# A third kind of expert pass in a mixture-of-experts kernel: the second block of at most 64 tokens holds its high and low parts side by side

## The reference, cut to what matters

```python
h = xb @ w_up[e] + b_up[e]                    # 1024 -> 2048
g = jnp.minimum(h[:, :D_FF], SWIGLU_LIMIT)
lin = jnp.clip(h[:, D_FF:], -SWIGLU_LIMIT, SWIGLU_LIMIT)
act = g * jax.nn.sigmoid(SWIGLU_ALPHA * g) * (lin + 1.0)
y = act @ w_down[e] + b_down[e]               # 1024 -> 1024
```

```
 76 208 143 145 198  80 185  99  48 294  84 119 154  72 229  41
 55 173  73  66  67 162 287  91  11 192 164  69 174  69 178  90
```

## Time and profile before

| | us |
|---|---|
| median of three runs | 2473.09 |
| profiled execution, its own time | 2474.64 |
| its span, first to last instruction | 2472.9 |
| of it: `experts`, about | 668 to 2440 |
| TensorE busy | 2277.4 (92%) |
| VectorE busy | 1678.7 (68%) |
| ScalarE busy | 1184.0 (48%) |

### The profile page before, as it was taken

The page is one execution under the profiler, slowest core; times in us unless marked ns, Lnnn a source line. Parts: engine busy times, 40 slices in busy tenths (PEclk is TensorE's granted clock), DMA queues, the critical chain, the costliest instruction groups (busy, mean ns, idle before and its releaser), DMA issues. The chain is left out here.

```text
span 2472.9 us, 32443 instructions
## 1 busy us (share of the span) xinstructions
PE 2277.4 (92%) x10850; PEld 1888.7 (76%) x10851; DVE 1678.7 (68%) x1915; ACT 1184.0 (48%) x1165; POOL 541.0 (22%) x539
## 2 busy tenths in 40 slices
PE   5999676889399999999999999999999999999993
PEld 4787665668278888888888888888888888888882
DVE  3688756646685555758679675967955796575764
ACT  3422132232164444647467464746744674464643
POOL 1001211103430011304124130413311331131402
PEclk9999867999599999999999999999999999999997
DMA  6123430541495566869789785978965896686964
GB/s 167 52 83 126 95 97 31 172 158 60 152 363 182 199 199 194 288 208 333 271 275 375 243 296 183 359 240 292 373 232 192 290 369 229 204 277 208 310 188 180
DMA packets 285809, 540.78 MB, mean 219 GB/s; under 512 B 37154, under 2 KB 53586, under 8 KB 284658
## 3 DMA queue, kind: packets, MB, share of 16 engines
q1 hardware_dynamic: 260306, 490.51, 57.5%
q0 software_dynamic: 25440, 49.47, 7.7%
HBM read 513.06 MB, written 64.57 MB: 234 GB/s over the span
## 5 line engine op out<-in xcount | busy, mean ns | idle before, releaser
L2286 DVE TENSOR_TENSOR ex_w_lo<-ex_raw,ex_w_hi 128x2048 fp32r<-128x2048 f32 x408 | 929.3, 2289 | 344.3 <-ACT ex_w_hi L2195 282.0
L2195 ACT CAST ex_w_hi<-ex_raw 128x2048 fp32r<-128x2048 f32 x371 | 711.1, 1917 | 402.4 <-PE ex_ps_l L2458 158.1
L2106 POOL TENSOR_TENSOR ex_passed<-ex_ident 128x1 f32<-128x1 f32 x136 | 96.0, 706 | 1299.7 <-ACT ex_y L2228 1270.8
L2451 PE MATMUL ex_ps_g<-ex_w_hi,ex_x_hi 128*128 128x512 f32 x784 | 309.5, 395 | 7.5 <-issue 7.5
L2451 PE MATMUL ex_ps_l<-ex_w_hi,ex_x_hi 128*128 128x512 f32 x784 | 308.1, 393 | 0.0
L2453 PE MATMUL ex_ps_g<-ex_w_hi,ex_x_lo 128*128 128x512 f32 x784 | 306.3, 391 | 0.0
L2452 PE MATMUL ex_ps_g<-ex_w_lo,ex_x_hi 128*128 128x512 f32 x784 | 306.1, 390 | 0.0
L2453 PE MATMUL ex_ps_l<-ex_w_hi,ex_x_lo 128*128 128x512 f32 x784 | 305.3, 389 | 0.0
L2452 PE MATMUL ex_ps_l<-ex_w_lo,ex_x_hi 128*128 128x512 f32 x784 | 305.2, 389 | 0.0
L2451 PE MATMUL ex_ps_y<-ex_w_hi,ex_h_hi 128*128 128x512 f32 x544 | 216.5, 398 | 0.0
L2453 PE MATMUL ex_ps_y<-ex_w_hi,ex_h_lo 128*128 128x512 f32 x544 | 212.3, 390 | 0.0
(11 more groups left out here) (436 smaller groups left out, 3779.2 us busy)
## 6 DMA issues: line engine op xcount, KB each, us to landing
ex_raw<-in_w_up_dram SPq DMA_DIRECT2D x272, 1024.0 KB, 9.5
ex_raw<-in_w_down_dram SPq DMA_DIRECT2D x136, 1024.0 KB, 9.6
st_tab<-tabs SPq DMA_DIRECT2D x8, 1408.0 KB, 12.0
pr_raw<-in_w_in_dram SPq DMA_DIRECT2D x10, 1024.0 KB, 5.7
tabs<-pr_x POOLq DMA_DIRECT2D x32, 256.0 KB, 2.3
por_raw<-in_w_out_dram SPq DMA_DIRECT2D x16, 256.0 KB
t<-mix_sig_o SPq DMA_DIRECT2D x8, 512.0 KB
fi_h<-h SPq DMA_DIRECT2D x8, 512.0 KB, 9.6
```

The lines of the kernel that those rows point to most:

```text
L2106: pool.tensor_tensor(passed[:, :], ident[:, 0:1], ident[:, 0:1], ALU.add).then_inc(passed_done, 1)
L2195: nc.scalar.copy(w_hi[:, j % SPLIT, :, :], raw[:, j % RAW, :, :]).then_inc(hi_done, 1)
L2286: v.tensor_tensor(w_lo[:, j % SPLIT, :, :], raw[:, j % RAW, :, :], w_hi[:, j % SPLIT, :, :].bitcast(F32), ALU.subtract).then_inc(lo_done, 1)
L2451: pe.matmul(to[:, :], hi_in[:, b, kk, :], w_hi[:, s, k, :], start=first, stop=False)
```

## The change

A third kind of pass is added, `small`, for an expert with 129 to 192 tokens (`SMALL` = 64; the last expert never takes it). `plan()` has two more steps, and its number now holds three bits for the kind and the pass number above them; `passes` has a third `If`, and with it a third body on every engine.

In a small pass the second block has at most 64 tokens. Its high parts stand in columns 0 to 63 of the stationary tile `x_hi` (and `h_hi`), its low parts in columns 64 to 127. One matmul with the high weight therefore gives high by high in rows 0 to 63 of the bank and low by high in rows 64 to 127; a second with the low weight adds high by low and low by low. That is two matmuls in place of three for each of the second block's tiles. The bias goes to rows 0 to 63 alone, through a second picker `pick[:, 1, :]` whose right half is zero.

The two halves are then added: `under_out` on ScalarE copies rows 64 to 127 of the bank to the tile `under`, and `fold` on VectorE adds `under` to rows 0 to 63 of the bank. This happens six times in a small pass: after chunks 1 and 5 (before the second block's sigmoid), after chunks 3 and 7 (before its clip), and after chunks 10 and 11 (before its part of `y_out`). The semaphores count in larger steps in the two old kinds of pass so that they agree.

```diff
+                    link(v.tensor_tensor(over[:, :], cnt_f[:, :], over_at[:, :], ALU.is_gt))
+                    link(v.scalar_tensor_tensor(plan_c[:, :], two[:, :], 2.0, plan_b[:, :], ALU.mult, ALU.add))
...
             with eng.If((plan & 1) > 0):
                 body(n, e, 2, plan)
+            with eng.If((plan & 4) > 0):
+                body(n, e, 2, plan, AHEAD, True)
             with eng.If((plan & 2) > 0):
                 body(n + (plan & 1), e, 1, plan)
...
+                def under_out(n, j, bank):
+                    act.wait_ge(chunk_used, n * CHUNKS + (USED + j + 1))
+                    nc.scalar.copy(under[:, j % 4 // 2 if j < 8 else j % 2, :], bank[SMALL:P, :]).then_inc(sig_done, 1)
...
                     for b in range(blocks):
                         act.wait_ge(y_free[b], n * 16 + 16)
+                        if small and b:
+                            act.wait_ge(hidden_done, n * 4 + (j - 7))
                         ins = nc.scalar.activation(y[:, b, col:col + 512], y_bank(j, b, blocks)[:, :], ACT.Copy,
...
+                        if small:
+                            v.tensor_tensor(x_hi[:, b, rows, SMALL:P],
+                                            ps_t[half][:, :].rearrange("p (k t) -> p k t", k=4)[:, :, 0:SMALL],
+                                            x_hi[:, b, rows, 0:SMALL].bitcast(F32), ALU.subtract).then_inc(
...
                 def choose(n, e):
+                    v.tensor_copy(pick[:, 1, 0:SMALL], keep["row_pick"][:, bass.ds(e, 1)].to_broadcast([P, SMALL]))
...
+                def fold(n, to, i, turn):
+                    v.wait_ge(sig_done, n * 8 + turn)
+                    return v.tensor_tensor(to[0:SMALL, :], to[0:SMALL, :], under[:, i, :], ALU.add)
...
+                def y_fold(n, j, blocks):
+                    fold(n, y_bank(j, 1, blocks), j % 2, j - 3).then_inc(hidden_done, 1)
...
                         if j in (6, 8):
+                            h_low(n, kind, j // 8, blocks, small)
+                        if small and j >= 10:
+                            y_fold(n, j, blocks)
...
                             pe.matmul(to[:, :], hi_in[:, b, kk, :], w_hi[:, s, k, :], start=first, stop=False)
+                            if small and b:
+                                mm = pe.matmul(to[:, :], hi_in[:, b, kk, :], w_lo[:, s, k, :], start=False,
+                                               stop=last)
+                                continue
                             pe.matmul(to[:, :], hi_in[:, b, kk, :], w_lo[:, s, k, :], start=False, stop=False)
                             mm = pe.matmul(to[:, :], lo_in[:, b, kk, :], w_hi[:, s, k, :], start=False, stop=last)
```

More of the change, by code:

```diff
@@ L30 @@
 PAIR = 2
+SMALL = 64
 SLOTS = BLOCKS * P
@@ L2134, in scatter, with one_pass @@
                             compute_op=ALU.add).then_inc(y_free[b], 16)
-                def one_pass(n, e, blocks, plan, kind=AHEAD):
+                def one_pass(n, e, blocks, plan, kind=AHEAD, small=False):
                     n = pool.snap(n)
@@ L2202, in x_high, with h_high @@
                                            t_hi, count_of(kind, blocks, i + half))
-                def h_high(n, kind, half, blocks):
+                def h_high(n, kind, half, blocks, small):
                     for b in range(blocks):
+                        rows = SMALL if small and b else P
                         i = h_turn_no(kind, half, blocks) + b
                         act.wait_ge(t_full, turned(n, kind, blocks, i))
-                        nc.scalar.copy(h_hi[:, b, 4 * half:4 * half + 4, :],
-                                       ps_t[i % 2][:, :].rearrange("p (k t) -> p k t", k=4)).then_inc(
+                        nc.scalar.copy(h_hi[:, b, 4 * half:4 * half + 4, 0:rows],
+                                       ps_t[i % 2][:, :].rearrange("p (k t) -> p k t", k=4)[:, :, 0:rows]).then_inc(
@@ L2217, in sigmoid @@
                         ins = nc.scalar.activation(glu[:, row(half, b, blocks), :], g_bank(half, b, blocks)[:, :],
                                                    ACT.Sigmoid, scale=ALPHA)
-                    ins.then_inc(sig_done, 1)
-                def y_out(n, j, read, blocks):
+                    ins.then_inc(sig_done, 1 if small else 2 + 4 * half)
+                def under_out(n, j, bank):
+                    act.wait_ge(chunk_used, n * CHUNKS + (USED + j + 1))
+                    nc.scalar.copy(under[:, j % 4 // 2 if j < 8 else j % 2, :], bank[SMALL:P, :]).then_inc(sig_done, 1)
@@ L2222, in y_out @@
+                def y_out(n, j, read, blocks, small):
                     act.wait_ge(chunk_used, n * CHUNKS + (USED + j + 1))
@@ L2295, in x_low, with h_low @@
                                             t_free, count_of(kind, blocks, i + half))
-                def h_low(n, kind, half, blocks):
+                def h_low(n, kind, half, blocks, small):
                     for b in range(blocks):
@@ L2455, in multiply, with item @@
                             if j == 1:
[L2456 removed]
+                                pe.wait_ge(bias_set, 3)
                             col = (j // 2) % 2 * F + (j // 4) * 512
[L2458 removed]
+                            mine = 1 if small and b else 0
+                            mm = pe.matmul(to[:, :], pick[:, mine, :], bias_hl[:, col:col + 512], start=False, stop=True)
                     mm.then_inc(chunk_used, 1)
[L2461 removed]
+                def item(n, kind, blocks, small=False):
                     for j in range(CHUNKS):
[L2463 removed]
+                        multiply(n, kind, j, blocks, small)
                         if j == 5:
```

133 lines of the change are left out of this document (79 added, 54 removed).

## The result

| | before | after |
|---|---|---|
| median of four runs, us | 2472.68 | 2455.18 |
| lowest to highest | 2470.59 to 2473.58 | 2452.26 to 2461.07 |
| ratio, 95% interval | | 0.9933, 0.9912 to 0.9955 |
| profiled execution, us | 2474.64 | 2461.07 |
| span, us | 2472.9 | 2459.2 |

The change gives 17.5 us of the 92 that were forecast. The time is above the range of the prediction (2369 to 2410).

The account below looks back on a forecast made before the run. TensorE was taken to bound the expert loop. From 2474.64 us profiled, 108.8 of matmuls came off, 16.4 of handover and 0.4 of plan steps were added: 2382.6, or 2381.1 us as median. Range 2369 to 2410, to hold 8 in 10.

Parts of the forecast that it names:

- the fetching of instructions: TensorE's jumps over bodies in the expert loop: no cost in the sum, as the jump over the pair body showed none.
- The sum: Whole program: 2474.64 - 108.8 + 16.4 + 0.4 = 2382.6 us profiled, 2381.1 us as median of the runs.
- Code: Rival: TensorE's larger loop no longer stays in place, one 1.24 us stop for each of 31 experts, 2420 us; 8%.
- what bounds the kernel: Expert loop, 731 to 2430 us: TensorE is the bound, busy 1693.05 of 1699 us at full clock.
- the count of passes: Expert loop: 19 single and 15 pair passes before; ten of the pairs become small passes.
- the pass: A small pass drops 48 matmuls of 0.2267 us, going from 70.90 to 60.0 us; ten passes save 108.8 us.
- the cover of 0.3 us: After chunk 7 of a small pass: a 4.0 us chain under 4.34 us of cover fits by 0.3, costing 0.
- the folds: Six `under_out` and six `fold` per small pass, about 0.65 us each; `fold` bounded between 0.4 and 1.3 us.
- the handover: End of a small pass: the next pass starts later, 1.8 us before singles and pairs, 1.0 before smalls; 16.4 us.
- a fold of 0.4 us: Low end of the forecast's own range: `fold` at 0.4 us was to give 2371 us.
- Slower than before: Rival: 62 jumps over loop bodies each stall; 1.24 us each gives 2458 us, above 1.48 each eats the gain; 3%.
- the prediction's signs: Small passes near 60.0 us, 480 fewer matmuls, some 16 us more TensorE waits, `fold` 0.69 us; "issue" gaps would mean code.

Follow-up runs that it names:

- shared: The changed kernel with one TensorE body for pair and small passes, the low tile's matmuls and bias under an If of their own; 2388.1 us, ratio 0.9658.
- dead282: The kernel before plus a never-run body of 282 matmuls between pair and single bodies, on TensorE alone; 2695.96 us, ratio 1.090.
- small_first: The changed kernel with TensorE's three bodies in the order small, pair, single; 2545.88 us, ratio 1.0288.
- never_small: The changed kernel with the threshold set so that the small body is never run; 2697.91 us, ratio 1.0919.
- dead282_end: The kernel before plus the never-run 282 matmuls on TensorE, placed behind the single body at the loop's end; 2482.87 us, ratio 1.0044.
- dead96: The kernel before plus a never-run body of 96 matmuls between pair and single bodies, on TensorE alone; 2480.65 us, ratio 1.0033.
- dead190: The kernel before plus a never-run body of 190 matmuls between pair and single bodies, on TensorE alone; 2485.6 us, ratio 1.0051.
- direct_y: The one-body version with the last two folds replaced: ScalarE scales the whole second block, then VectorE adds the scaled low half to `y`; 2372.13 us, ratio 0.9597.
- small_last: The changed kernel with TensorE's three bodies in the order pair, single, small; 2412.28 us, ratio 0.9755.

## Why the prediction was wrong, step by step

The step that failed is the fetching of instructions. The sum puts it at nothing, because the jump over the pair body costs nothing before the change, and the rival "Code" prices a stop at 1.24 us. Found are five stops of 4.2 to 14.7 us behind the pair passes (51.2 us), 7.8 us more at the loop's entry and about 15 us of lower clock and restart behind the stops. The other terms held to about 5 us in sum.

**Right: what bounds the kernel, and the count of passes.** Ten small passes, 480 matmuls less. TensorE stayed the bound.

**Right: the pass.** Two small passes in succession start 61.70 us apart; less the 1.55 us wait in it, 60.15 against the predicted 60.0.

```profile
879.04 1.04 PE L2459 MATMUL ex_ps_t<-ex_ident,ex_x_rows 128*128 128x128 f32 x8
...
884.39 0.50 PE L2508 MATMUL ex_ps_g<-ex_w_hi,ex_x_hi 128*128 128x512 f32 x1 [1.55 <-DVE ex_x_hi L2321]
...
940.74 1.04 PE L2459 MATMUL ex_ps_t<-ex_ident,ex_x_rows 128*128 128x128 f32 x8
```

In that stretch of a small pass VectorE is busy 43 of 62 us and TensorE 60.45, and no wait for chunk 7's product stands in it: the cover of 0.3 us held.

```profile
875.00:937.00 62.00, 60.45 (x283) 50.06 (x282) 42.99 (x40) 34.37 (x35) 9.04 (x10) 1.00 0.69 226
```

**Right: the folds.** By tile and line, VectorE's `fold` on the last bank and ScalarE's `under_out` from it (shortest/median/longest ns):

```profile
L2238 ACT COPY ex_under<-ex_ps_l x30: 582/582/585, 839.3 to 2383.4; 64x512 f32<-64x512 f32 x30
...
L2351 DVE TENSOR_TENSOR ex_ps_l<-ex_ps_l,ex_under x30: 683/692/692, 840.0 to 2385.0; 64x512 f32<-64x512 f32 x30
```

0.69 and 0.58 us, against 0.65 each. So adding into PSUM on 64 partitions takes VectorE what reading 128 partitions of it took before; these rows don't tell the two effects apart.

**Right in kind, small by a quarter: the handover.** At the end of expert 2's small pass the chain is the one that was worked out: the subtraction ends, then the fold, then the second `y_out`.

```profile
879.24 0.58 ACT L2238 COPY ex_under<-ex_ps_l 64x512 f32<-64x512 f32 x1 [0.65 <-PE ex_ps_l L2510]
...
881.55 0.69 ACT L2249 ACTIVATE ex_y<-ex_ps_l,ex_scatter_at 128x512 f32<-128x512 f32 x1 [1.01 <-DVE ex_ps_l L2351]
```

```profile
878.62 2.29 DVE L2313 TENSOR_TENSOR ex_w_lo<-ex_raw,ex_w_hi 128x2048 fp32r<-128x2048 f32 x1 [2.61 <-ACT ex_w_hi L2207]
880.83 0.68 DVE L2351 TENSOR_TENSOR ex_ps_l<-ex_ps_l,ex_under 64x512 f32<-64x512 f32 x1
```

What reached TensorE: 2.08 us at a pair (1.8 predicted), 1.55 at a second small pass (1.0), and about 1.95 at a single (1.8), spread over the first weight that chunk 8 needs, 0.30, `h_lo`, 1.34, and the product, 0.61 less the 0.29 of any single:

```profile
1154.01 0.50 PE L2508 MATMUL ex_ps_y<-ex_w_hi,ex_h_hi 128*128 128x512 f32 x1 [1.34 <-DVE ex_h_lo L2341]
...
1157.64 0.66 PE L2469 MATMUL ex_ps_t<-ex_ident,ex_lin 128*128 128x128 f32 x4 [0.61 <-DVE ex_lin L2377]
```

20.5 us in all instead of 16.4. That a second small pass's copies and subtractions are half as long bought only 0.5 of the 0.8 us that it was credited with.

**Right: the sum of these.** shared has all of these terms and no stops, and its profiled execution is 2390.81 against the 2382.6 of the sum. Of the 8.2 us between, about 4 are waits (25.4 in its rows above, 20.7 more than before, against 16.4) and about 4 are not assigned. One figure of the prediction has no working: with a fold of 0.4 us in place of 0.65 its own chain gives about 5 us less, 2376, and not 2371. `fold` measured 0.69, so nothing hangs on it.

**Wrong: the rival "Code", its price and its chance.** The prediction named the mechanism and what would show it, gaps for "issue" on TensorE. Three things in the working failed. That the time lies 3 us from the 2458 of its rival "Slower than before" is luck: that is 62 stops of 1.24 us, and there are five, long ones.
- The price. One stop was taken at 1.24 us, from behind the loop, and called the longest of its kind in the trace. It isn't: the stop at the loop's entry, 6.24 us in the row above, is in the 7.5 us of the earlier trace rows, and a packet of instructions comes within it. In the loop of the kernel after the five stops are 13.77, 14.70, 4.21, 14.06 and 4.42 us. In the turn of the loop that holds the stop from 1015.6 to 1030.3 (944 to 1030 us) the queue shows 8 packets, against 1 in the 114 us before it; by smaller stretches one packet comes in 964 to 974, one in 994 to 1004, one in 1004 to 1014 while TensorE works, and five in 1014 to 1030 (two as the stop begins, two about 8 us into it, one 13 us into it): a long stop is several fetches one behind the other. The two 4 us stops come in turns with as many packets. Behind expert 9, from 1206 to 1316 us, there are nine, but three of them come while the single pass runs (1275 to 1311 us) and none within the stop of 4.21 us. So a single pass between the jump and the next expert hides most of the fetching. Taking the row of 1.24 us for the price of any stop was the error of size: with the lower clock behind it a long stop costs 16 to 17 us.
- The place. It was put at "each expert", 31 times or 62. It comes behind a pass of one kind: behind each pair pass here, each of 15 in dead282, each of the ten small passes in small_first.
- The evidence against. "Today the jump over the pair body costs nothing visible" was a true reading (3 packets in 1659 us), but of a loop that stays in place, and it was used for a loop that might not. It says nothing about the price once a block has to be fetched in each turn. The reading that was to be had instead: the three packets of the earlier trace rows all come in the first pair pass (731 to 793 us), and none after it until 2395 us, which means that the loop before is held whole, and a change that adds 57% of code to it puts just that at stake. 8% for the milder case was too little for a state that no row showed.

**What each of the prediction's signs said.** Pass periods, the count of matmuls, the waits for VectorE and the 0.69 us all came as told. Only "issue" gaps told of the miss, as the prediction says they would.

**Code, as far as it is settled.** An estimate of TensorE's loop from records, a matmul and a weight load each: 660 instructions for the pair body, 334 for the single, 565 for the small. Shown: never-run code is enough (dead282, never_small); between 190 and 282 dead matmuls in the middle there is an edge; the same 282 at the end cost 9 us; the order of three bodies moves the time by 134 us; without a second copy of the body there is one stop of 1.5 us behind the first pair pass and no other (shared). So it is neither size alone nor the jump alone. My reading, argued only: while the loop runs through a long body, blocks are read ahead in order, those behind the body's end too, though they are then jumped over; with one block too many in a turn each of them pushes out one that the next pass needs. In dead282_end the blocks behind the dead body are not reached in this way. Which blocks these are, and how bodies fall on block borders, stays open; no kernel here shifted the loop by a few instructions to try it.

The Trainium skill, "Advanced Engine Details and Errata", ISA Cache, gives TensorE 128 KB in lines of 16 KB. As an estimate from that page of the Trainium skill and the counts above, at 64 bytes an instruction, the loop is 64 KB before, 76 in dead96, 88 in dead190, and 100 in dead282 and after, all under 128. These counts leave out waits, branches and register instructions, which no record shows. In dead282's pair passes a packet comes for about every 225 records, so by the Trainium skill's 256 instructions to 16 KB the four are nearer 72, 84, 96 and 108 KB, an estimate too, and still under 128. The packets of dead282 (2.72 MB in 166) have the 16 KB of the Trainium skill's page, and nine in a turn would be one more than eight lines hold; that agrees, but dead282_end, with the same 100 KB, doesn't fetch them. The Trainium skill, "Runtime: NRT & Kernel Launch", Instruction fetch mechanics, says that a taken branch out of the current window of two pages stalls for a fetch. The loop before, dead96 and shared, which jump over more than that at every second expert without a stop, speak against two pages on TensorE. That a jump can stall for a fetch agrees with the five packets within a long stop.

## What to carry to other kernels

A new kind of pass is also a new body in the loop, and its price can be larger than all its arithmetic: before adding one, look at the instruction packets in the loop's stretch, and if there are nearly none, take it that the loop is held whole and that this can end. The count of packets afterwards does not give the price; the waits for "issue" do. Where two kinds differ in few instructions, give them one body with the difference under a condition (here 67 us), and if there must be two, try their order. A step that waits in the middle of an in-order engine's hand-over between passes is paid at each pass in full; moving the addition behind the engine's own work (direct_y) won back 16 of 20 us.

## What the runs showed of the hardware that was not expected

- A body of 282 matmuls that is never run, in the middle of TensorE's loop, cost 223 us in 2472; the same body at the loop's end cost 9 us.
- A stop for instructions behind a pass of the loop is 11.6 to 16.2 us where four to six packets come one behind the other within it, 3 to 4.4 us in milder cases (small_last, dead190, two of the kernel after), and 1.5 us in dead96 and shared. At the loop's entry it is 6.2 to 14.6 us, and behind the loop, where the loop itself has no such stops, 1.24 to 2.1.
- small_last fetches 51 packets in the loop's stretch with stops of 3.2 to 4.0 us, the kernel after 47 with stops of up to 14.7: the count of fetches does not tell the cost.
- After a stop of 13 to 15 us without matmuls TensorE is granted 0.62 to 0.82 of its clock for the next 8 us (dead282 and the kernel after), and its matmuls there are 0.43 us apart instead of 0.2267. In dead282 that is about 25 us over 15 stops.
- VectorE adds into PSUM, 64 partitions of 512 columns, in 0.69 us, the time in which it reads 128 partitions of them. It also reads a bank's rows 64 to 127 beside an operand and a result in partitions 0 to 63 (direct_y).
